# Ten places instead of eight for the expert weights of a two-block transformer kernel

## The reference, cut to what matters

```python
def expert_choice_moe(h, w_router, w_gate, w_up, w_down):
    cap = max(1, CAPACITY_FACTOR * S // N_EXPERTS)            # 32 tokens for each of 16 experts
    aff = jax.nn.softmax(jnp.einsum('bsd,de->bse', h, w_router), axis=-1)
    gate, idx = lax.top_k(aff.transpose(0, 2, 1), cap)
    xin = jax.vmap(lambda hb, ib: hb[ib])(h, idx)
    hid = jax.nn.silu(jnp.einsum('becd,edf->becf', xin, w_gate)) * jnp.einsum('becd,edf->becf', xin, w_up)
    y = jnp.einsum('becf,efd->becd', hid, w_down) * gate[..., None]
    return jnp.zeros_like(h).at[bidx, idx].add(y)
```

## Time and profile before

| | |
|---|---|
| median of 3 runs | 1680.14 us (1678.73 to 1680.47) |
| the profiled execution, its own time | 1679.07 us |
| its span in the profile | 1677.3 us |
| mean granted clock of PE | 0.935 of 2.4 GHz |
| PE busy | 1588.4 us, 95% of the span |
| DVE, ACT, POOL busy | 812.5, 680.6, 48.0 us |
| moved by DMA | 400.19 MB, mean 239 GB/s |

### The profile page before, as it was taken

How to read it: one execution, slowest core, us unless ns; L and a number is a source line. 1 busy time by engine, 2 the same in 40 slices (tenths; PEclk the granted TensorE clock), 3 DMA queues, 4 the chain that set the end, 5 groups by cost and what they waited for, 6 DMA issues and landing times.

```text
span 1677.3 us, 26700 instructions
## 1 busy us (share of the span) xinstructions
PE 1588.4 (95%) x10902; PEld 1320.2 (79%) x10902; DVE 812.5 (48%) x1093; ACT 680.6 (41%) x749; POOL 48.0 (3%) x38
## 2 busy tenths in 40 slices
PE   7996879999999988899999999999999999999998
PEld 7895755555555544799999989999899989899997
DVE  4679631111111111555556766555655556766554
ACT  5563231212121212544345655343643454753343
POOL 0006200000000000000000000000000000000000
PEclk9898967878787879899999999999999999999999
DMA  7632479999999999665555336554555546346552
GB/s 235 178 101 76 171 322 429 426 429 428 429 428 428 429 428 428 237 205 196 177 175 176 126 126 221 180 185 166 179 195 179 186 139 202 125 149 203 181 194 75
DMA packets 164073, 400.19 MB, mean 239 GB/s; under 512 B 5752, under 2 KB 136232, under 8 KB 151592
## 3 DMA queue, kind: packets, MB, share of 16 engines
q1 hardware_dynamic: 162824, 397.74, 63.7%
q10 hardware_dynamic: 1184, 1.57, 0.3%
HBM read 398.23 MB, written 1.06 MB: 238 GB/s over the span
## 4 chain that ended last, share of the span: by engine, by line
PE 80%; DVE 7%; DMA 6%; ACT 3%; issue 3%; POOL 0%; SPq 0%; ACTq 0%; DVEq 0%; POOLq 0%
PE ps L573 12%; PE ps L574 12%; PE ps L575 12%; PE ps L804 10%; PE ps L598 6%; PE ps L599 6%; PE ps L600 6%; PE ps L792 5%; PE ps L812 4%; DMA ring<-w_expert_up 4%; PE ps L853 3%; DMA ring<-w_in 2%; ACT w1h_sb L1117 1%; DVE ring L1557 1%; DVE w1l_sb L1505 1%
## 5 line engine op out<-in xcount | busy, mean ns | idle before, releaser
L1787 DVE TENSOR_TENSOR wl_sb<-raw_sb,wh_sb 128x2048 fp32r<-128x2048 f32 x162 | 371.0, 2292 | 322.8 <-ACT wh_sb L1259 322.5
L573 PE MATMUL ps<-xTh_sb,wh_sb 128*128 128x256 f32 x1696 | 482.4, 284 | 9.1 <-DVE xTl_sb L1459 5.7
L574 PE MATMUL ps<-xTl_sb,wh_sb 128*128 128x256 f32 x1696 | 479.9, 283 | 0.0
L575 PE MATMUL ps<-xTh_sb,wl_sb 128*128 128x256 f32 x1696 | 479.8, 283 | 0.0
L1259 ACT ACTIVATE wh_sb<-raw_sb 128x2048 fp32r<-128x2048 f32 x162 | 310.3, 1916 | 322.3 <-PE ps L575 319.2
L573 PEld LDWEIGHTS ps<-xTh_sb,wh_sb 128*128 128x128 f32 x1696 | 325.2, 192 | 12.5 <-DVE xTl_sb L1459 7.0
L574 PEld LDWEIGHTS ps<-xTl_sb,wh_sb 128*128 128x128 f32 x1696 | 325.3, 192 | 1.5
L575 PEld LDWEIGHTS ps<-xTh_sb,wl_sb 128*128 128x128 f32 x1696 | 325.3, 192 | 0.0
L804 PE MATMUL ps<-ring,work 128*32 128x512 f32 x1152 | 155.6, 692 | 7.3 <-DMA ring<-w_expert_up 7.2
L598 PE MATMUL ps<-wh_sb,hidh_sb 128*128 128x512 f32 x384 | 151.2, 394 | 1.2 <-DVE wl_sb L1787 1.2
L599 PE MATMUL ps<-wl_sb,hidh_sb 128*128 128x512 f32 x384 | 149.9, 390 | 0.0
(11 more groups left out here) (303 smaller groups left out, 1826.9 us busy)
## 6 DMA issues: line engine op xcount, KB each, us to landing
ring<-w_expert_gate SPq DMA_DIRECT2D x24, 2048.0 KB, 20.7
ring<-w_expert_up SPq DMA_DIRECT2D x24, 2048.0 KB, 22.2
ring<-w_expert_down SPq DMA_DIRECT2D x24, 2048.0 KB, 27.7
raw_sb<-ffn_gate SPq DMA_DIRECT2D x44, 1024.0 KB, 5.2
raw_sb<-ffn_up SPq DMA_DIRECT2D x44, 1024.0 KB, 5.2
raw_sb<-ffn_down SPq DMA_DIRECT2D x44, 1024.0 KB, 4.7
raw_sb<-w_in SPq DMA_DIRECT2D x22, 1024.0 KB, 5.2
ring<-w_in SPq DMA_DIRECT2D x16, 1024.0 KB, 5.8
```

The lines of the kernel that those rows point to most:

```text
L573: pe.matmul(to, w_h[:, k, fs], x_h[:, k, :], start=k == 0, stop=False)
L574: pe.matmul(to, w_h[:, k, fs], x_l[:, k, :], start=False, stop=False)
L575: mm = pe.matmul(to, w_l[:, k, fs], x_h[:, k, :], start=False, stop=k == KD - 1)
L1787: dve.tensor_tensor(wl[j], raw[j], wh[j].bitcast(F32), ALU.subtract).then_inc(raw_free[j], 1)
```

## The change

Two slots more, so NS is 10. One is `x_place`, the place of `x_sb` and `xT_sb` together. The other lies in `work`, over the place of `fin_row`, `prm_all` and `tb_raw`; only the four small tables keep a place of their own behind it. To make the router's tiles fit, `topw`, `chosen`, `place` and `ones_e` are laid over `g4` and `u4`. The slots are put in another order (ring, ring, work, work, ring, ring, work, ring, ring, x's place). What SP issues first is reordered to that, `prm_all` is loaded behind the last half, SP's loop has 30 halves a turn and PE's has five experts, with the sixteenth written out behind it.

```diff
+        with nc.sbuf_tensor("x_place", [P, SLOT], F32) as x_place:
+            pass
         x_sb = sb("x_sb", TT * D)
...
-        t2 = region(work, WORK - LATE + D)
+        t2 = region(work, WORK - 3 * (TBW + 1) - 2 * DH)
...
-        g4, u4 = [t2(FE).rearrange("p (k q) -> p k q", k=KD) for _ in range(2)]
+        g4u4 = t2(2 * FE)
+        g4, u4 = [g4u4[:, FE * i:FE * i + FE].rearrange("p (k q) -> p k q", k=KD) for i in range(2)]
+        topw, chosen, place, ones_e = [g4u4[0:NE, S * i:S * i + S] for i in range(4)]
...
-        slots = [ring[:, s * SLOT:s * SLOT + SLOT] for s in range(6)] + [t2(SLOT) for _ in range(2)]
+        in_ring, in_work = [ring[:, s * SLOT:s * SLOT + SLOT] for s in range(6)], [t2(SLOT) for _ in range(3)]
+        slots = in_ring[0:2] + in_work[0:2] + in_ring[2:4] + in_work[2:3] + in_ring[4:6] + [x_place[:, :]]
...
             half(1, 0, 1)
             sp.wait_ge(sem["o_put"], TT)
             sp.wait_ge(sem["ho_put"], TT)
-
-            sp.dma_start(prm_all, prm_in.rearrange("l p n -> p l n")).then_inc(sem["late_in"], 16)
+            half(2, 0, 2)
+            half(3, 0, 3)
+
             sp.dma_start(tb_future, future).then_inc(sem["late_in"], 16)
             sp.dma_start(tb_onehot, onehot).then_inc(sem["late_in"], 16)
             sp.dma_start(tb_rel, relb).then_inc(sem["late_in"], 16)
             sp.wait_ge(sem["w1_lo"], W1)
-            half(2, 0, 2)
+            half(4, 0, 4)
+            half(0, D, 6)
             sp.wait_ge(sem["acc_done"], 1)
-            for i in range(3, 6):
-                half(i, 0, i)
-            for i in range(2):
-                half(i, D, 6 + i)
+            half(5, 0, 5)
+            half(1, D, 7)
+            half(2, D, 8)
+            sp.wait_ge(sem["route"], LOGITS)
+            sp.wait_ge(sem["xn_done"], 2)
+            half(3, D, 9)
...
-            TURN = 4 * 6
             with sp.Fori(0, (NE * 6 - NS) // TURN) as g:
                 for j in range(TURN):
-                    next_half(NS + j, sp.snap(TURN * g + j + 1), sp.snap(4 * D * g + D * ((NS + j) // 6)))
+                    next_half(NS + j, sp.snap(TURN * g + j + 1), sp.snap(TURN // 6 * D * g + D * ((NS + j) // 6)))
             for q in range(NS + (NE * 6 - NS) // TURN * TURN, NE * 6):
                 next_half(q, q - NS + 1, D * (q // 6))
+            sp.wait_ge(sem["half_used"], NE * 6 - NS + 1)
+            sp.dma_start(prm_all, prm_in.rearrange("l p n -> p l n")).then_inc(sem["late_in"], 16)
...
-            pe.wait_ge(sem["late_in"], 64)
+            pe.wait_ge(sem["late_in"], 48)
             pe.matmul(bank(3)[0:2 * DH, 0:TBW + 1], tb_rel, tb_onehot, start=True, stop=True).then_inc(sem["tb_ps"], 1)
...
-            with pe.Fori(0, NE // 4) as g:
-                for i in range(4):
+            with pe.Fori(0, NE * 6 // TURN) as g:
+                for i in range(TURN // 6):
                     expert(g, i)
+            expert(NE * 6 // TURN, 0)
...
-            act.wait_ge(sem["late_in"], 64)
             act.wait_ge(sem["tb_out"], 16)
+            act.wait_ge(sem["half_used"], NE * 6 - NS + 1)
             nc.scalar.dma_start(tb_raw, bass.AP(tb_dram, 0, [[1, P], [TBW + 1, 2 * DH], [1, S]])).then_inc(sem["tb_in"], 16)
...
+                dve.wait_ge(sem["late_in"], 64)
                 dve.tensor_scalar(prm, prm_all[:, bass.ds(L, 1), :].rearrange("p l n -> p (l n)"), 1.0, None, ALU.mult)\
                     .then_inc(sem["prm_ready"], 1)
...
-            pool.wait_ge(sem["half_used"], 6 * (NE - 1))
+            pool.wait_ge(sem["half_used"], 6 * (NE - 1) + 2)
             for j in range(3):
                 pool.memset(hold[:, 1 + j:2 + j], 0.0).then_inc(raw_free[j], 1)
-            pool.wait_ge(sem["half_used"], 6 * (NE - 1) + 3)
+            pool.wait_ge(sem["half_used"], 6 * NE)
```

More of the change, by code:

```diff
@@ L257, in two_blocks @@
         r_mx, r_nm, r_sum, r_rec = t2(TT), t2(TT), t2(TT), t2(TT)
-        topw, chosen, place, ones_e = [t2(S)[0:NE, :] for _ in range(4)]
         top8 = t2(8)[0:NE, :]
@@ L336, in pf @@
             return prm[:, a:b] if i is None else prm[:, a + i:a + i + 1]
-        names = """x_in0 x_in1 const_in one_in band_in mask_in w1_in0 w1_in1 w1_hi w1_lo ex_in0 ex_in1 ex_in2 ex_in3 ex_in4 ex_in5 ex_in6 ex_in7
+        names = """x_in0 x_in1 const_in one_in band_in mask_in w1_in0 w1_in1 w1_hi w1_lo ex_in0 ex_in1 ex_in2 ex_in3 ex_in4 ex_in5 ex_in6 ex_in7 ex_in8 ex_in9
             mxT_ps k_scaled late_in tb_out tb_in raw_in0 raw_in1 raw_in2 fin_out
@@ L345, in two_blocks @@
             sc_ps sc_nm sc_exp sc_cnt eT_ps eT_act eT_dve o_ps o_put ho_ps ho_sq ho_ms ho_std ho_put gs_done
-            masks_zero lg_ps lg_nm lg_exp route_done route_ps hot_done xin_ps
+            masks_zero route hot_done xin_ps
             xe_ready hote_done half_used n0_ps used0 used1 used2 back_ps g4_done u4_done back_done fold_ps esil_done ehid_done
@@ L355, in two_blocks @@
         w1_in = [sem["w1_in0"], sem["w1_in1"]]
-        ex_in = [sem["ex_in0"], sem["ex_in1"], sem["ex_in2"], sem["ex_in3"], sem["ex_in4"], sem["ex_in5"], sem["ex_in6"], sem["ex_in7"]]
+        ex_in = [sem["ex_in0"], sem["ex_in1"], sem["ex_in2"], sem["ex_in3"], sem["ex_in4"], sem["ex_in5"], sem["ex_in6"], sem["ex_in7"],
+                 sem["ex_in8"], sem["ex_in9"]]
         raw_in = [sem["raw_in0"], sem["raw_in1"], sem["raw_in2"]]
@@ L394, in two_blocks @@
         Z_READ = [sem["z_" + name] for name, _, _ in PROJ]
+        LOGITS, MAXIMA, EXPS, WEIGHTS, WEIGHTS_TURNED, PLACES, PLACES_TURNED = range(1, 8)
+        TURN = 30
         W1_IN = 2 * len(PROJ)
@@ L773, in _ @@
                                    start=k == 0, stop=k == KD - 1)
-            mm.then_inc(sem["lg_ps"], 1)
-            pe.wait_ge(sem["late_in"], 64)
+            mm.then_inc(sem["route"], 1)
+            pe.wait_ge(sem["late_in"], 48)
             pe.matmul(bank(3)[0:2 * DH, 0:TBW + 1], tb_rel, tb_onehot, start=True, stop=True).then_inc(sem["tb_ps"], 1)
-            pe.wait_ge(sem["route_done"], 1)
+            pe.wait_ge(sem["route"], WEIGHTS)
             for t in range(TT):
                 mm = pe.transpose(bank(1)[0:NE, t * P:t * P + P], aff[:, t, :], ident)
-            mm.then_inc(sem["route_ps"], 1)
-            pe.wait_ge(sem["route_done"], 2)
+            mm.then_inc(sem["route"], 1)
+            pe.wait_ge(sem["route"], PLACES)
             for t in range(TT):
                 mm = pe.transpose(bank(2)[:, t * NE:t * NE + NE], place[:, t * P:t * P + P], ident[0:NE, 0:NE])
-            mm.then_inc(sem["route_ps"], 1)
+            mm.then_inc(sem["route"], 1)
             GATE_PS, UP_PS = 0, 2
@@ L817, in value @@
                 def value(per, v):
-                    return pe.snap(per * g + v)
+                    return per * g + v if isinstance(g, int) else pe.snap(per * g + v)
                 def landed(q):
@@ L823, in e_th @@
                 def e_th(per, v):
-                    return value(4 * per, per * i + v)
+                    return value(TURN // 6 * per, per * i + v)
                 q = 6 * i
@@ L1235, in _ @@
             nc.scalar.activation(hold[:, 5:6], ident[:, 0:1], ACT.Exp)
-            act.wait_ge(sem["lg_nm"], 1)
+            act.wait_ge(sem["route"], MAXIMA)
             for t in range(TT):
@@ L1239, in _ @@
                                          bias=r_nm[:, t:t + 1], accum_out=r_sum[:, t:t + 1])
-            a.then_inc(sem["lg_exp"], 1)
+            a.then_inc(sem["route"], 1)
             with act.Fori(0, NE) as e:
@@ L1287, in ffn @@
                 step(0, STEPS - 1, last=True)
-            act.wait_ge(sem["late_in"], 64)
             act.wait_ge(sem["tb_out"], 16)
+            act.wait_ge(sem["half_used"], NE * 6 - NS + 1)
             nc.scalar.dma_start(tb_raw, bass.AP(tb_dram, 0, [[1, P], [TBW + 1, 2 * DH], [1, S]])).then_inc(sem["tb_in"], 16)
             act.wait_ge(sem["half_used"], 6 * NE)
-            nc.scalar.dma_start(fin_row, fin_w).then_inc(sem["late_in"], 16)
+            nc.scalar.dma_start(fin_row, fin_w).then_inc(sem["const_in"], 16)
             with act.Fori(0, DEPTH2) as L:
@@ L1713, in _ @@
                 .then_inc(sem["xn_done"], 1)
-            dve.wait_ge(sem["lg_ps"], 1)
+            dve.wait_ge(sem["route"], LOGITS)
             ch.link(dve.tensor_reduce(r_mx, bank(0)[:, 0:TT * NE].rearrange("p (t e) -> p t e", t=TT), AX.X, ALU.max))
-            dve.scalar_tensor_tensor(r_nm, r_mx, -1.0, n_rstd, ALU.mult, ALU.mult).then_inc(sem["lg_nm"], 1)
-            dve.wait_ge(sem["lg_exp"], 1)
+            dve.scalar_tensor_tensor(r_nm, r_mx, -1.0, n_rstd, ALU.mult, ALU.mult).then_inc(sem["route"], 1)
+            dve.wait_ge(sem["route"], EXPS)
             ch.link(dve.reciprocal(r_rec, r_sum))
@@ L1720, in _ @@
                 v = dve.tensor_scalar(aff[:, t, :], aff_e[:, t, :], r_rec[:, t:t + 1], None, ALU.mult)
-            v.then_inc(sem["route_done"], 1)
-            dve.wait_ge(sem["route_ps"], 1)
+            v.then_inc(sem["route"], 1)
```

(7 more changed lines are left out.)

## The result

| | median | lowest to highest | runs | span of the profiled execution |
|---|---|---|---|---|
| before | 1679.91 us | 1678.12 to 1682.98 | 20 | 1677.3 us |
| the change | 1683.76 us | 1681.58 to 1686.56 | 20 | 1680.2 us |

The change is slower: ratio 1.0024, 95% interval 1.0018 to 1.0031. The forecast was 1673.2 and a range up to 1677.2, so both the sign and the range were wrong. The medians are 3.9 us apart; the profiled executions (1679.07 and 1682.03 us) show 2.9 us of difference in the span.

A forecast was written before the change was run, and what follows sets the result against it. The expert stage was taken to end on the weight stream, 6.9 us later than PE alone would. All cost terms were zero, so 1680.14 - 6.9 = 1673.2 us; range 1670.3 to 1677.2.

The forecast's parts named there:

- PE's loop of five experts and one written out behind it: Expert stage on PE: 0.02 us per jump back, two jumps for three, so zero; ends 0 and 0.1.
- the slower rival: Parameters land late at DVE's new wait, holding the next stage's start; at 25 us of transfer, 1686.8 us; chance 0.03.
- the parameters: 817 KB loaded behind half 95, landing by 670 to 675, before DVE copies them at 679.6; zero, cover 5 to 9 us.
- PE, not the stream, bounds the stage: Expert stage: with later halves landing 9.8 us earlier, the whole stage becomes PE's; gain 6.9 us.
- the waits are to be priced by ends and not by their sum: PE's expert stage: compare end 690.40 with undisturbed 683.5, giving 6.9 us, rather than adding 8.8 us of waits.
- the fill ends by 239: Initial loading of ten halves ends about 237.0 to 239, before the first slot release at 243.2.
- The small tables: Router: three tables PE needs at 220.77 now lie behind halves 2 and 3, ending near 209; zero, 11 us cover.
- SP's new wait: SP waits for logits and xn_done before half 9; only the bias table's store and the loop stand behind; zero.
- the raw pieces: First two raw pieces land behind half 95 and the parameters, at 675; ACT splits them at 679; zero, cover 4 us.
- the release by POOL: POOL releases the split buffers with the last half, not three halves earlier; three one-column memsets run beside ACT's work; zero.
- half 93 has 3.1 us to spare: Fourth half of expert 15 lands at 658.4, PE wants it at 661.5; called the tightest one.
- one more expert of 29.2 us may come: Clock rival in PE's expert stage: one more slow expert cuts the gain to 5.2 us, 1674.9 us; chance 0.14.

The follow-up runs named there:

- the written-out kernel: The changed kernel (ten slots) with PE's sixteen experts written out, no loop: 1671.74 us, ratio to before 0.9953; again on another chip 1669.95 us, 0.9946.
- ten slots, one jump: The changed kernel with PE's loop run for two turns of five experts and the last six written out: 1677.39 us, ratio to before 0.9988.
- the loop of eight: The kernel before (eight slots) with PE's loop made two turns of eight experts instead of four of four: 1683.07 us, and 1682.85 us again.

## Why the prediction was wrong

**The step that failed** is the one on "PE's loop of five experts and one written out behind it", which I put at zero, "ends 0 and 0.1". The bound came from a jump that costs 0.02 us, but it was the jump of a loop of four, and I carried it over to a loop of another length. That row couldn't bound it: whether code is still there at a jump depends on how much there is. Measured, the two jumps are worth 12 us in time (1671.7 to 1683.8), or 9.9 us in the profiled stages (444.4 to 454.3). No rival had it; the slower rival stood on the parameters, which were in time. With the wrong term the sum gave -6.9; with the measured one it would have been -6.9 + 9.9 = +3.0, against 2.9 in the spans and 3.9 in the medians.

**Point by point.** That PE, not the stream, bounds the stage once ten halves lie ready: right. That the waits are to be priced by ends and not by their sum: right, 444.2 forecast and 444.4 measured without the jumps, and the gain over before in time was then 8.4 us (1680.17 beside those runs, to 1671.74), the rest of it being the earlier start of that kernel's stage, 237.55 for 239.35, which nothing in the forecast gave. That the fill ends by 239, before the first refill: right. The small tables, SP's new wait, the parameters, the raw pieces and the release by POOL at nothing: right; 986.8 us lie behind the stage in the written-out kernel, 986.9 before. That half 93 has 3.1 us to spare: too much. In the written-out kernel the weight loads of PE waited 0.6 us for a half, at 659.54, which is 418.1 us after the first refill (241.42) and not 415.2 as the forecast has it. The 3 us less fit the 3 us that nine slots show between a loop that is kept and written-out code, so it is probably the code that is read that took the reserve; with ten slots and no code read it wasn't run. That one more expert of 29.2 us may come: it didn't. The kernel before has two of them (experts 2 and 9, of which the forecast names the second), the changed one two (2 and 7) and the written-out one two (3 and 10). The lower end of the range was added up wrong by 0.2 us: 1671.5 less 1.4 is 1670.1 and not 1670.3.

The rule of the Trainium skill (TensorE: Matmul & The Clock Gate, HAM oscillation) that I set against the rows, by which waits let the clock fall, was rightly left out of the sum. The written-out kernel has none of the 8.8 us of waits, and its stage is 6.6 us shorter, not more than 8.8. In the changed kernel a stretch with stalls again shows the higher mean clock, 0.88 and 0.83 for 0.81. But behind three of the six jumps in a long loop the clock did fall: behind the stall of 3.24 us (ten slots, one jump) and those of 2.84 and 2.82 us (the two runs of the loop of eight) the granted clock was 0.50, from 381.7, 464.4 and 465.8 on. The first 31 products behind the first of them took 5.29 us and the first 30 behind the last 5.33, for 3.63 behind the stalls of 2.68 to 2.74 us.

## What to carry to other kernels

The length of a loop body is a resource like a tile. A loop over slots must hold a common multiple of the slots and of an expert's six halves: 24 halves with eight slots, 18 with nine, 30 with ten. When a body grows for such a reason, look at what the longer body costs at its jump back before you count the gain, and take the price from a loop of the same length or not at all. Here three ways out were measured: write the loop out (the version that beats both, 1671.7 and 1670.0), take a slot number with a shorter pattern (nine, 1673.7), or pay. And when a stall has no releaser in a profile, compare the number of instruction transfers and when they start, and look at which instruction stands behind the stall.

## What the runs showed of the hardware that I had not expected

PE reads a loop's code again where the body is five, six or eight of these experts, 1700, 2040 or 2720 matmuls and weight loads, and doesn't where it is three or four, 1020 or 1360. With the loops kept the page counts 42 instruction transfers of 16 KB. Written out it counts 58, and with a long loop 58 and two more for each jump: 60 with one (four runs), 62 with two. So a long loop gains nothing over written-out code: each turn is read as if it were new. A jump back into code that isn't there stood for 2.68 to 3.24 us, and in three of six cases a second time for 1.7 to 2.0 us behind 30 of the products (a fourth time for 0.2 us), while the weights held the DMA engines at 426 GB/s in the changed kernel; code that lies straight ahead cost no stall at all. In all six cases one instruction transfer started within 0.6 us of the end of the expert before the jump and a second 5.6 to 6.1 us behind the first. PE stood for the second one where its products ran at the upper clock, and hardly or not at all where they ran at the lower. The Trainium skill (Runtime: NRT & Kernel Launch) gives PE's instruction memory as 128 KiB, 2048 instructions, filled in blocks of 16 KiB, and calls the crossing of a block mostly hidden. The blocks of 16 KB and the hidden crossing straight ahead agree with the runs. An estimate from that section's 256 instructions in a block: 16 more transfers for 12 more experts are some 341 instructions an expert, about 1700 for a loop of five. By the size alone that would have fitted, and here it didn't: the measurement decides. The same section also says that a taken branch to code outside the two blocks of the current window must fetch it before the engine can go on. The stalls at the long jumps agree; the loop of four doesn't: it is over five such blocks long, and was turned without a transfer or a stall.

The code that is read also delays the weights: with 16 to 18 more instruction transfers (0.3 MB) half 87 or 93 was 3 us later after the first refill in the profiles of eight slots, and half 93 with nine, though 0.3 MB at 428 GB/s is 0.7 us. Why it is more than their bytes wasn't tried.
